# Sliding attention: scores and values of two head pairs in one block every second step, scores ahead of values, shares ahead of the next softmax

## What is computed

```python
def swa_mixer(h, kb, vb, w_q, sinks, rel_table, w_out):
    B, T, _ = h.shape
    NB = T // BLOCK
    q = (h @ w_q).reshape(B, NB, BLOCK, SWA_KV_HEADS, SWA_GROUP, SWA_HEAD_DIM)
    s = jnp.einsum('bnqhgd,bnkhd->bnhgqk', q, kb).astype(jnp.float32) * (SWA_HEAD_DIM ** -0.5)
    ...
    s = jnp.where(mask[None, :, None, None], s + bias, NEG)
    m = jnp.maximum(jnp.max(s, axis=-1, keepdims=True), sink)
    p = jnp.exp(s - m)
    p = p / (jnp.sum(p, axis=-1, keepdims=True) + jnp.exp(sink - m))
    o = jnp.einsum('bnhgqk,bnkhd->bnqhgd', p.astype(vb.dtype), vb)
    return o.reshape(B, T, SWA_Q_HEADS * SWA_HEAD_DIM) @ w_out
```

## Time and profile before

| | us |
|---|---|
| median of 3 runs | 971.37 |
| lowest and highest | 971.07, 972.6 |
| profiled execution, its whole time | 971.38 |
| its span, first to last instruction | 969.6 |
| busy in the span: PE, DVE, ACT, POOL | 961.7, 659.9, 492.1, 59.1 |
| chain that ended last: share of PE | 97% |
| mean granted TensorE clock | 0.999 |

### The profile page before, as it was taken

The page is one execution under the profiler, slowest core; times in us unless marked ns, Lnnn a source line. Parts: engine busy times, 40 slices in busy tenths (PEclk is TensorE's granted clock), DMA queues, the critical chain, the costliest instruction groups (busy, mean ns, idle before and its releaser), DMA issues.

```text
span 969.6 us, 13082 instructions
## 1 busy us (share of the span) xinstructions
PE 961.7 (99%) x5366; PEld 826.8 (85%) x5366; DVE 659.9 (68%) x934; ACT 492.1 (51%) x589; POOL 59.1 (6%) x128
## 2 busy tenths in 40 slices
PE   9999999999999999999999999999999999999997
PEld 8888888888889878888888889988888888888886
DVE  5877786555669967656666659867766766666665
ACT  5555554444447855444444445465554544454454
POOL 3451000000001001000000013000000000000000
PEclk9999999999999999999999999999999999999999
DMA  8664767677463326767765556453266465655551
GB/s 256 210 196 133 223 179 226 219 198 219 174 217 102 117 89 192 223 195 213 202 209 205 188 161 218 139 191 126 73 236 207 152 217 175 199 191 181 190 193 54
DMA packets 115251, 176.57 MB, mean 182 GB/s; under 512 B 5548, under 2 KB 78200, under 8 KB 115192
## 3 DMA queue, kind: packets, MB, share of 16 engines
q1 hardware_dynamic: 115016, 175.54, 56.3%
q10 hardware_dynamic: 176, 0.20, 0.1%
HBM read 174.03 MB, written 1.70 MB: 181 GB/s over the span
## 4 chain that ended last, share of the span: by engine, by line
PE 97%; ACT 1%; DMA 1%; DVE 0%; issue 0%; POOL 0%; SPq 0%; ACTq 0%; DVEq 0%
PE ps L368 94%; PE ps L372 3%; DMA raw<-in_a_w_in 1%; ACT RR L2153 0%; ACT whi L2153 0%; DVE RR L1243 0%; SPq L2940 0%; ACT xs L2150 0%; DVE M L1235 0%; POOL st L2764 0%; POOL whi L2804 0%; ACT M L2153 0%; DVE dg L1239 0%; DVE M L2130 0%; DVE x L1235 0%
## 5 line engine op out<-in xcount | busy, mean ns | idle before, releaser
L368 PE MATMUL ps<-whi,RR 128*128 128x512 f32 (+1 forms) x1556 | 397.6, 387 | 0.0
L1235 DVE TENSOR_TENSOR wlo<-raw,whi 128x1024 fp32r<-128x1024 f32 (+1 forms) x323 | 373.7, 1199 | 27.6 <-ACT whi L2153 27.4
L2153 ACT ACTIVATE whi<-raw 128x2048 fp32r<-128x2048 f32 (+1 forms) x161 | 301.4, 1874 | 164.5 <-PE ps L368 136.1
L368 PEld LDWEIGHTS ps<-whi,RR 128*128 128x128 f32 x1556 | 283.8, 188 | 55.5 <-issue 0.9
L368 PE MATMUL ps<-RR,whi 128*128 128x512 f32 (+1 forms) x1264 | 261.1, 350 | 0.1
L368 PEld LDWEIGHTS ps<-RR,whi 128*128 128x128 f32 x1264 | 200.5, 190 | 27.3 <-issue 1.5
L368 PE MATMUL ps<-wlo,RR 128*128 128x512 f32 (+1 forms) x778 | 220.5, 385 | 0.0
L368 PEld LDWEIGHTS ps<-wlo,RR 128*128 128x128 f32 x778 | 144.2, 188 | 29.5 <-DVE wlo L1235 0.2
L1235 DVE TENSOR_TENSOR M<-M,ps 128x512 f32<-128x512 f32 (+1 forms) x57 | 38.8, 683 | 172.1 <-ACT M L2153 167.8
L368 PEld LDWEIGHTS ps<-RR,wlo 128*128 128x128 f32 x1016 | 138.4, 191 | 9.1 <-DVE wlo L1235 0.7
L368 PE MATMUL ps<-RR,wlo 128*128 128x256 f32 x1016 | 144.6, 282 | 0.0
(11 more groups left out here) (109 smaller groups left out, 418.9 us busy)
## 6 DMA issues: line engine op xcount, KB each, us to landing
raw<-in_w_up SPq DMA_DIRECT2D x32, 1024.0 KB, 6.2
raw<-in_w_down SPq DMA_DIRECT2D x32, 1024.0 KB, 5.6
raw<-in_w_ff SPq DMA_DIRECT2D x32, 1024.0 KB, 5.1
raw<-in_w_in SPq DMA_DIRECT2D x23, 1024.0 KB, 5.0
raw<-in_a_w_in SPq DMA_DIRECT2D x10, 1024.0 KB, 5.4
raw<-in_a_w_out SPq DMA_DIRECT2D x4, 1024.0 KB, 5.1
raw<-in_b_w_q SPq DMA_DIRECT2D x4, 1024.0 KB, 5.5
raw<-in_b_w_out SPq DMA_DIRECT2D x4, 1024.0 KB, 5.1
```

What stands on the lines that cost most here:

```text
L368: return pe.matmul(out, lhsT, rhs, start=start, stop=stop, skip_group_check=True)
L1235: return dve.tensor_tensor(out, a, b, op)
L2153: return act.activation(out, in_, ACT.Copy, **k)
```

## The change

PE: scores of two pairs go one behind the other every second step (0 and 1 ahead of the first query product, then 2 and 3, 4 and 5, 6 and 7), the even pair in banks 0 and 1, the odd one in banks 2 and 3; values of two pairs likewise, behind the scores of their step. Pairs 0 and 1, and 2 and 3, write their values into the two halves of one bank, which is filled and read as one tile. Each step still holds the transposes of one pair, now first. The query tiles and the values get other banks (`Q_BANKS`, `PV_BANKS`), the turned values' projection bank 6. ACT: the turned shares get a third buffer, and `highs` come in twos every second step (one copy of 512 columns for pairs 0 and 1, one for 2 and 3); `exps` and `ev_q` keep their places in it. DVE: `shares(i-1)` ahead of `soft(i)` in every step, and `lows` in twos likewise.

```diff
--- before.py
+++ after.py
@@ -222,7 +222,7 @@
         return self.M[:, 2816 + 768 * (p % 3):3584 + 768 * (p % 3)].rearrange("p (h k) -> p h k", h=2)
 
     def sw_v(self, p):
-        return self.M[:, 5120 + 768 * (p % 2):5888 + 768 * (p % 2)].rearrange("p (h k) -> p h k", h=2)
+        return self.M[:, 6912 + 768 * (p % 3):7680 + 768 * (p % 3)].rearrange("p (h k) -> p h k", h=2)
 
     def di_s(self, c):
 
@@ -258,6 +258,10 @@
 STEPS = [(p, c) for p in range(2) for c in range(2)]
 
 PLACES = ({1: (0, 128), 2: (128, 256), 0: (256, 512)}, {0: (0, 256), 1: (256, 384), 2: (384, 512)})
+
+Q_BANKS = {2: 4, 3: 5, 4: 4, 5: 5, 6: 5, 7: 4}
+
+PV_BANKS = {0: 4, 2: 5, 4: 2, 5: 3, 6: 2, 7: 3}
 
 HALVES = [(0, 0), (0, 512), (4, 0), (4, 512)]
 
@@ -305,6 +309,20 @@
         else:
             runs.append([m, 1, col, None])
     return [(m, n, dil, col, kind == "next") for m, n, col, kind in runs]
+
+
+def pv_tile(p):
+    return "pv", p if p > 3 else p // 2
+
+
+def pv_cols(p):
+    a = 0 if p > 3 else 256 * (p % 2)
+    return slice(a, a + 256)
+
+
+def pv_parts(oT, p):
+
+    return [part[:, p:p + (1 if p > 3 else 2), :].rearrange("p k t -> p (k t)") for part in oT]
 
 
 def by_parity(a):
@@ -878,7 +896,7 @@
 
     def scores(p):
         tile = ("sc", p)
-        take(tile, 0, 1)
+        take(tile, *((2, 3) if p % 2 else (0, 1)))
         kv = p // 4
         w_ = K.pair(tile, 384)
         for w in due(q_ready(p), K.empty(("kk",)) if kv else K.at("kt_first")):
@@ -902,10 +920,12 @@
         t.then_inc(*K.filled(tile))
 
     def values(p):
-        tile = ("pv", p)
+        tile, cols = pv_tile(p), pv_cols(p)
         v = V.sw_v(p)
         kv = p // 4
-        w_ = take(tile, 2 + p % 2)[:, 0:256]
+        if cols.start == 0:
+            take(tile, PV_BANKS[p])
+        w_ = K.bank(tile)[:, cols]
         for w in due(K.empty(("pt", p)), K.empty(("kv",))):
             pe.wait_ge(*w)
         v0, v1 = V.VW[:, 0, 64 * kv:64 * kv + 64], V.VW[:, 1, 64 * kv:64 * kv + 64]
@@ -916,10 +936,11 @@
             mm(w_[rows[h], 128:256], v0, v[:, h, 128:256], True, False)
         for h in range(2):
             t = mm(w_[rows[h], 128:256], v1, v[:, h, 256:384], False, True)
-        t.then_inc(*K.filled(tile))
+        if p > 3 or p % 2:
+            t.then_inc(*K.filled(tile))
 
     def v_turned():
-        b = take(("kv",), 2)
+        b = take(("kv",), 6)
         for w in due(K.empty(("vt",))):
             pe.wait_ge(*w)
         for c in range(2):
@@ -929,26 +950,26 @@
     def window():
 
         scores(0)
-        yield
         scores(1)
+        yield
         v_turned()
-        for i in range(1, 10):
+        for i in range(2, 11):
             yield
-            if i == 1:
-                turned(0)
-            if i < 7:
+            if i < 10:
+                turned(i - 2)
+            if i % 2 == 0 and i < 8:
+                scores(i)
                 scores(i + 1)
-            if 1 < i < 9:
-                turned(i - 1)
-            if i > 1:
-                values(i - 2)
+            if i % 2 == 0 and i > 2:
+                values(i - 4)
+                values(i - 3)
 
     def q_products():
         for f in (256, 512, 768):
             j, hi, lo = block(A["b_w_q"][0][:, f:f + 256], 8, 256)
             for i in range(2):
                 tile = ("q", f // 128 + i)
-                b = take(tile, 4 + i)
+                b = take(tile, Q_BANKS[tile[1]])
                 t = weights_stand(b[:, 0:256], j, hi, lo, cols[i], hT, range(8), h_ready(2), True, True)
                 t.then_inc(*K.filled(tile))
                 yield
@@ -966,7 +987,7 @@
                 if (k0, n, c) == (4, 1, 1):
                     norm_early(3)
                 t = weights_move(K.bank(tile), j, hi, lo, slice(0, 512), o_parts, slice(c * 128, c * 128 + 128),
-                                 range(k0, k0 + 4), k0, lambda k: K.empty(("pv", k)), k0 == 0, k0 == 4)
+                                 range(k0, k0 + 4), k0, lambda k: K.empty(pv_tile(k)), k0 == 0, k0 == 4)
                 if k0:
                     t.then_inc(*K.filled(tile))
                 elif c:
@@ -1741,25 +1762,23 @@
                 *K.up("sw_p", (p, h)))
 
     def lows(p):
+        tile, (hi, lo) = pv_tile(p), pv_parts(oT, p)
         for w in due(K.at("pv_hi", p)):
             dve.wait_ge(*w)
-        tt(oT[1][:, p, :], K.bank(("pv", p))[:, 0:256], oT[0][:, p, :].bitcast(F32), ALU.subtract).then_inc(
-            *K.emptied(("pv", p)))
+        tt(lo, K.bank(tile)[:, 0:256 if p > 3 else 512], hi.bitcast(F32), ALU.subtract).then_inc(*K.emptied(tile))
 
     def window():
 
         for i in range(11):
 
-            if i == 1:
-                shares(0)
+            if 0 < i < 9:
+                shares(i - 1)
             if i < 8:
                 soft(i)
-            if 3 < i:
+            if i % 2 == 0 and i > 2:
+                lows(i - 4)
+            if i in (8, 10):
                 lows(i - 3)
-            if 1 < i < 9:
-                shares(i - 1)
-            if i == 3:
-                lows(0)
             yield
 
     def halves(n):
@@ -2450,14 +2469,15 @@
 
     def turned(p):
         tile = ("pt", p)
-        for w in due(K.full(tile), *([K.full(("pv", p - 2))] if p >= 2 else [])):
+        for w in due(K.full(tile), *([K.full(pv_tile(p - 3))] if p >= 3 else [])):
             act.wait_ge(*w)
         copy(V.sw_v(p), K.pair(tile, 384)).then_inc(*K.emptied(tile))
 
     def highs(p):
-        for w in due(K.full(("pv", p))):
+        tile = pv_tile(p)
+        for w in due(K.full(tile)):
             act.wait_ge(*w)
-        copy(oT[0][:, p, :], K.bank(("pv", p))[:, 0:256]).then_inc(*K.up("pv_hi", p))
+        copy(pv_parts(oT, p)[0], K.bank(tile)[:, 0:256 if p > 3 else 512]).then_inc(*K.up("pv_hi", p))
 
     def ev_q(p):
         for w in due(K.full(("q", p))):
@@ -2469,7 +2489,9 @@
         for i in range(11):
             if 2 <= i < 10:
                 turned(i - 2)
-            if 3 <= i:
+            if i % 2 == 0 and i > 2:
+                highs(i - 4)
+            if i in (8, 10):
                 highs(i - 3)
             if i < 8:
                 exps(i)
```

More of the change, by code:

```diff
@@ L931, in window @@
         scores(0)
+        scores(1)
         yield
-        scores(1)
         v_turned()
-        for i in range(1, 10):
+        for i in range(2, 11):
             yield
-            if i == 1:
-                turned(0)
-            if i < 7:
+            if i < 10:
+                turned(i - 2)
+            if i % 2 == 0 and i < 8:
+                scores(i)
                 scores(i + 1)
-            if 1 < i < 9:
-                turned(i - 1)
-            if i > 1:
-                values(i - 2)
+            if i % 2 == 0 and i > 2:
+                values(i - 4)
+                values(i - 3)
     def q_products():
```

## The result

| | before | with the change |
|---|---|---|
| median of 6 runs, us | 971.96 | 978.89 |
| lowest, highest | 971.07, 972.77 | 977.99, 979.53 |
| profiled execution, its whole time | 971.38 | 979.52 |
| its span | 969.6 | 977.8 |
| stage: first scores to the sixth projection product | 53.09 | 59.69 |

The account below looks back on a forecast made before the run. TensorE, busy 961.7 of 969.6 us, was taken as the bound. Waits of 8.6 us less 2.8 for grouping gave 5.8, from the chain 5.7: 971.4 + 5.7 = 977.1 us, own range 974.8 to 979.0, wide range 974.5 to 980.5.

Parts of the forecast that it names:

- The chain of DVE and ACT: Sliding-attention stage: soft, exps, shares and query copies added up in the new order, setting when scores 3, 5, 7 start.
- The waits: PE waits before scores 3, 5, 7 and in the first projection product: 3.3 + 2.8 + 1.8 + 0.7 = 8.6 us.
- rival B: Slower still: PE's clock falls to 1.2 GHz in a wait, adding 3.4 us, 980.5 us in all; chance 0.07.
- the odd scores coming a product early: Scores 3, 5, 7 move ahead one product, their query tiles do not; PE waits 3.3 us before scores 3.
- the alternation: Shares(i-1) ahead of soft(i): DVE waits for exponentials, ACT for maxima; DVE idles some 2.1 us before shares 1, 3, 5, 7.
- Rival A: Faster: odd scores do not wait and grouping shows in full, 971.4 - 2.8 = 968.6 us; chance 0.06.
- the condition of rival A: It decides at whether ACT's copy ev_q(3) is over by 315.1; the trace has it at 318.26.
- Grouping: Joining scores and values in pairs on PE saves about 0.4 us a block, 2.8 us in all, bounds 2.4 to 3.2.
- The tail: From four matmuls into the first projection product to the fifth product's end: 18.4 us after the change, 20.25 before.
- a clock below 1.00 in the stretch: Sign of being wrong: the granted clock in the sliding-attention stage below 1.00 in the new profile.
- the step that called a fall unlikely: Behind the last matmul the clock held for some 3.8 us idle; longest wait here 3.3, so rows speak against a fall.
- Not touched: Weight blocks covered by over 10 us, no DMA issued elsewhere, everything behind the stage shifted by the same 5.7 us.

Follow-up runs that it names:

- e6: The changed kernel with unneeded matmuls filling PE's waits before scores 3, 5 and 7 (12, 4, 6); stage 58.55 us, median 976.44 us, ratio 1.0044.
- e1: The kernel before with one edit: VectorE makes shares(i-1) ahead of soft(i), no grouping; stage 60.80 us, median 978.88 us, ratio 1.0069.
- e3: The changed kernel with ScalarE copying query tile i+2 ahead of exps(i), from step 1 on; stage 61.15 us, median 979.29 us, ratio 1.0083.
- e2: The changed kernel with the VectorE order undone, soft(i) ahead of shares(i-1); stage 57.71 us, median 975.81 us, ratio 1.0044.
- e7: e2 with 12 unneeded matmuls in PE's wait before scores 3; stage 56.10 us, median 975.11 us, ratio 1.0035.
- e4: The changed kernel with the edits of e2 and e3 together; stage 57.39 us, median 975.84 us, ratio 1.0042.
- e5: e4 with scores ahead of transposes in the two steps of scores 4, 5 and 6, 7; stage 53.04 us, median 971.17 us, ratio 0.9993.
- e8: e5 with shares(i-1) ahead of soft(i) on VectorE again; stage 60.41 us, median 980.08 us, ratio 1.0085.

## Why the prediction held, point by point

**Sign and size.** Slower, 5.7 forecast, 6.6 measured in the stage, 6.9 by the medians. By places, measured from the first scores: scores 3 at 12.39 us (forecast 12.46), scores 5 at 24.03 (24.10), scores 7 at 36.26 (36.35). The chain of DVE and ACT, added up from rows 5 and 6 of a kernel in which it never ran in this order, was right within 0.1 us three times. The starts of soft(2) and soft(3) agree too (13.35 and 19.25 us in, forecast 13.36 and 19.25), so this is no luck of the sum.

**The waits.** 3.3 forecast before scores 3, 3.2 measured by the starts. Before scores 5 I had 2.8 and the starts give 1.3 (331.57 - 329.55 - 0.76): the slow clock took up the rest without moving scores 5, as rival B had it there (a cost of 0.1; e6 shows none). Before scores 7: 1.8 and 1.9.

**What moved where.** The account of the cause was too broad. I put the odd scores coming a product early first, as what PE waits for, and the alternation second. e1 shows that the alternation alone is enough for the whole loss, and e3 that with the query tiles in time nothing is gained as long as the engines alternate. But it is not the only thing that costs time: with it undone the change still costs 4.6 us (e2), 3.0 at full clock (e7), by the odd scores that wait and by scores that stand behind transposes (e4). The costs do not add up; each hides behind the other. Rival A was said to decide at whether `ev_q(3)` is over by 315.1; e3 brings the query tiles in time and still isn't faster, so that point didn't decide. A needed the order on DVE undone too (e4), and the scores moved (e5), and even then DVE's own work left no more than 0.46 us to gain. This step of the prediction, the condition of rival A, failed; the forecast did not rest on it.

**Grouping.** 2.8 us forecast with bounds 2.4 to 3.2, about 2.3 by the starts (e5). Two values in one block cost 364.34 - 359.95 - 2.72 = 1.67 us, against 2 x 1.03 for two single ones: 0.4 saved, as estimated. Two scores save less. I priced one scores by the step of 5.64 us from 321.20 to 326.84; the steps beside it in the kernel before take 5.54 and 5.55:

```profile
315.66 2.18 PE L368 MATMUL ps<-RR,whi 128*128 128x256 f32 x16
...
332.39 2.17 PE L368 MATMUL ps<-RR,whi 128*128 128x256 f32 x16
```

The step that I took holds about 0.1 us of waiting, so one scores costs 0.93 instead of 1.03 and joining two saves 0.3 instead of 0.4, which makes the sum 2.4 (4 x 0.3 + 4 x 0.4, less the same 0.4). The forecast of the kernel's time hardly changes by it, as the waits took up what PE saved. Transposes alone between products came to 0.76 (356.47 to 359.95, less 2.72), where I had 0.70. The rule of the Trainium skill (TensorEngine Tiling (Array Packing), Key Properties: a change of tiling mode drains TensorE) agrees with these rows. Taken alone it points to rival A, a faster kernel, which did not come, because PE was not what set the stage's pace in the new order.

**The tail.** From four matmuls into the first projection product 18.4 us were forecast; from the release of lows(2), 348.85 + 0.19, to 367.23 it is 18.2.

**The clock, the term that was mis-sized.** lows(2) was done at 41.3 us into the stage instead of 40.2. The prediction had named a clock below 1.00 in the stretch as a sign of being wrong, and on the clock it was wrong. Rival B was the mechanism, at 0.07, and it did occur, behind scores 3 and behind scores 7. Its price was 3.4 and it cost 1.1 (e6), since I let a whole product run at half the clock on top of the values, and the slow stretch was over by 348.5. What failed is the step that called a fall unlikely: it drew on one idle stretch, behind the last matmul, where the clock held for some 3.8 us; here PE sat idle 3.03 and 1.73 us by the profile, and it fell behind both. That the time still came out in the forecast's own range, by 0.1 us, is in part luck: the next wait hid the first fall whole, and the second cost 1.1 us.

**Not touched.** Weight blocks, DMAs and all behind the stage: no wait of PE in the changed kernel's list names a weight block or a DMA behind the first 10 us (its weight loads wait 0.9 us in all for low parts, the same as before and none of it in the stage), and the distance to before is constant, 8.15 us, from the stage to the end.

## What to carry to other kernels

When two engines hand a small thing to and fro (softmax on one, exponentials on the other), the order in which one of them takes up the next item decides whether they overlap or alternate; add up one round for each order before touching the pieces of the engine that looks like the bound. A wait that is removed where the profile shows it is a gain only if the chain behind it moves: ask what set the releaser's time, and test by restoring that alone. Time saved on the busiest engine is worth little in a stretch in which another engine, here DVE with no gap for 30 us, is already just in time: 2.3 us saved, 0.05 gained.

## What the runs showed of the hardware

**The clock.** A fall of the granted clock need not show in the wait itself: in the changed kernel it is 1.00 in 316 to 319 with PE idle for two thirds, still 1.00 up to 320.5, PE having resumed at 319.93, and 0.50 from 321 to 324. In e8 it came earlier: 0.50 in 326.0 to 326.5, with PE resuming at 326.58. And the length of a wait alone did not tell whether it fell: it fell behind waits of 3.03 and 1.73 (the change), 3.18 (e1), 3.03 (e2), 3.37 and 2.52 (e3), 2.11 (e4) and at the end of 2.86 (e8), and not behind 1.74 (e1) or 2.91 (e8). The two waits of e8:

```profile
325.00:333.00 8.00, 6.42 (x42) 5.14 (x43) 5.80 (x17) 4.69 (x14) 0.20 (x1) 0.57 0.42 133
345.00:352.00 7.00, 4.09 (x21) 3.35 (x21) 6.86 (x17) 4.46 (x11) 0.20 (x1) 1.00 0.06 13
```

A fall cost 1.1 us (e6, two of them) and 1.6 us (e7, one) of the stage. The Trainium skill, TensorE: Matmul & The Clock Gate, section HAM oscillation, says that waits between matmuls put the clock back; the runs agree. They add that in a stage bound by another engine the next wait can absorb a fall: the first of the changed kernel cost nothing (11.64 us from scores 3 to scores 5, 11.63 in e6), while the second, which slowed the values that lows(2) waits for, cost the 1.1 us.

**Idle time of PE in brackets.** Where PE waits, the profile's idle time is about 0.2 us short of what the starts give (3.03 against 3.20), because the end of the last matmul is modelled. In a stage with many short waits, some too short for a bracket, the sum of brackets, 1.5 us in e5, was about half of the 2.8 us by the starts.
